# Residual gates of a two-layer hybrid diffusion step: turned to rows, kept in DRAM and read back to every partition, in place of products against the identity

## What is computed

```
for l in range(2):
    mp = split(silu(c_ctx) @ ada_w[l] + ada_b[l], 6)     # group 0: shift, scale, gate, shift, scale, gate
    ms = split(silu(c)     @ ada_w[l] + ada_b[l], 6)     # group 1
    m_p = token_mixers(modulate(xp, mp[0], mp[1]), ...)  # conv and attention, merged, @ w_out
    xp  = layer_norm(ALPHA * xp + mp[2] * m_p, ln1_g[l], ln1_b[l])
    # the same for xs with ms
    f_p = swiglu(...) if l == 0 else moe_swiglu(...)     # of modulate(xp, mp[3], mp[4])
    xp  = layer_norm(ALPHA * xp + mp[5] * f_p, ln2_g[l], ln2_b[l])
```

## Time and profile before

| | us |
|---|---|
| median of 3 runs (lowest, highest) | 1244.71 (1243.43, 1245.07) |
| the profiled execution, whole | 1244.88 |
| its span, first to last instruction | 1243.1 |
| PE busy in the span | 1142.6 |
| DVE, ACT, POOL busy | 853.1, 714.9, 127.9 |
| mean granted TensorE clock, share of full | 0.961 |

### The profile page before, as it was taken

How to read it: one execution, slowest core, us unless ns; L and a number is a source line. 1 busy time by engine, 2 the same in 40 slices (tenths; PEclk the granted TensorE clock), 3 DMA queues, 4 the chain that set the end, 5 groups by cost and what they waited for, 6 DMA issues and landing times.

```text
span 1243.1 us, 15877 instructions
## 1 busy us (share of the span) xinstructions
PE 1142.6 (92%) x5645; PEld 906.7 (73%) x5645; DVE 853.1 (69%) x1203; ACT 714.9 (58%) x1022; POOL 127.9 (10%) x132
## 2 busy tenths in 40 slices
PE   5699999999899999899999999469999999999980
PEld 1466667888788888766667887458888888888870
DVE  1575657756575455696657666449889889889965
ACT  1444445644644444544445644348888888888862
POOL 5030000001270000440000001240000000000001
PEclk7799999999999999999999999779999999999995
DMA  9799986554369656478775644079999999999952
GB/s 329 280 365 330 319 315 237 203 170 136 119 201 412 233 185 188 137 269 300 262 265 194 227 145 132 5 277 366 374 379 384 377 381 384 372 384 381 377 203 101
DMA packets 165849, 332.57 MB, mean 268 GB/s; under 512 B 6528, under 2 KB 27120, under 8 KB 165792
## 3 DMA queue, kind: packets, MB, share of 16 engines
q1 hardware_dynamic: 158288, 307.78, 70.2%
q0 software_dynamic: 7472, 24.03, 5.7%
q10 hardware_dynamic: 32, 0.01, 0.0%
HBM read 314.48 MB, written 17.30 MB: 267 GB/s over the span
## 4 chain that ended last, share of the span: by engine, by line
PE 84%; ACT 5%; DVE 4%; DMA 3%; issue 2%; POOL 0%; ACTq 0%; SPq 0%; DVEq 0%; POOLq 0%
PE bank L1302 24%; PE bank L1304 23%; PE bank L1303 23%; PE bank L1497 4%; ACT w_hi L556 2%; DMA raw<-in_ada_w 1%; PE bank L1560 1%; PE bank L1392 1%; PE bank L1578 1%; DVE xT_lo L873 1%; PE bank L1452 1%; PE bank L1568 1%; ACT work L574 1%; DVE w_lo L838 1%; ACT xT_hi L579 1%
## 5 line engine op out<-in xcount | busy, mean ns | idle before, releaser
L838 DVE TENSOR_TENSOR w_lo<-raw,w_hi 128x1024 fp32r<-128x1024 f32 (+1 forms) x492 | 571.4, 1190 | 195.7 <-ACT w_hi L556 193.7
L556 ACT ACTIVATE w_hi<-raw 128x1024 fp32r<-128x1024 f32 (+1 forms) x504 | 500.7, 1008 | 314.6 <-PE bank L1304 314.5
L1302 PE MATMUL bank<-w_hi,xT_hi 128*128 128x512 f32 (+1 forms) x1056 | 414.3, 392 | 18.4 <-DVE w_lo L838 12.3
L1304 PE MATMUL bank<-w_lo,xT_hi 128*128 128x512 f32 (+1 forms) x1056 | 402.8, 381 | 0.0
L1303 PE MATMUL bank<-w_hi,xT_lo 128*128 128x512 f32 (+1 forms) x1056 | 402.1, 381 | 0.0
L1302 PEld LDWEIGHTS bank<-w_hi,xT_hi 128*128 128x128 f32 x1056 | 200.1, 190 | 62.4 <-issue 14.2
L1304 PEld LDWEIGHTS bank<-w_lo,xT_hi 128*128 128x128 f32 x1056 | 198.9, 188 | 35.8
L1303 PEld LDWEIGHTS bank<-w_hi,xT_lo 128*128 128x128 f32 x1056 | 199.5, 189 | 30.8
L1302 PE MATMUL bank<-w_hi,hT_hi 128*128 128x512 f32 x360 | 141.7, 394 | 0.0
L1304 PE MATMUL bank<-w_lo,hT_hi 128*128 128x512 f32 x360 | 140.6, 390 | 0.0
L1303 PE MATMUL bank<-w_hi,hT_lo 128*128 128x512 f32 x360 | 140.3, 390 | 0.0
(11 more groups left out here) (234 smaller groups left out, 897.9 us busy)
## 6 DMA issues: line engine op xcount, KB each, us to landing
raw<-in_w_in SPq DMA_DIRECT2D x52, 1024.0 KB, 7.3
raw<-in_ada_w SPq DMA_DIRECT2D x48, 1024.0 KB, 7.6
raw<-in_moe_w_gate SPq DMA_DIRECT2D x32, 1024.0 KB, 7.3
raw<-in_moe_w_up SPq DMA_DIRECT2D x32, 1024.0 KB, 7.9
raw<-in_moe_w_down SPq DMA_DIRECT2D x32, 1024.0 KB, 7.7
raw<-in_moe_w_gate SPq DMA_DIRECT2D x16, 768.0 KB, 8.6
raw<-in_moe_w_up SPq DMA_DIRECT2D x16, 768.0 KB, 7.2
raw<-in_moe_w_down SPq DMA_DIRECT2D x16, 768.0 KB, 7.6
```

The source lines that it names most:

```text
L556: nc.scalar.activation(w_hi[:, unit, 0:n], raw[:, r, at:at + n], ACT.Copy).then_inc(hi_done, 1)
L838: V.tensor_tensor(w_lo[:, unit, 0:n], raw[:, r, at:at + n], w_hi[:, unit, 0:n].bitcast(F32), ALU.subtract).then_inc(lo_done, 1)
L1302: pe.matmul(o, hi, wh, start=start, stop=False)
L1304: return pe.matmul(o, hi, wl, start=False, stop=stop)
```

## The change

The gate columns of a layer are turned once, by four products with the eight columns of `adaT` of one vector and one group as the stationary operand (8x128 out, all four into bank 0). ACT copies the 8x512 result to `ada_rows[0:8, 0, :]`. POOL writes it to a new DRAM tensor `gate_rows` (four rows of 1024 for a layer), waits for that, and reads each row back to all 128 partitions of its `gate_bc` tile: two reads for n = 2l when the keys and values are stored, two for n = 2l + 1 when `merged` has come twice. DVE's two residual steps wait for these reads in place of the ACT copies. The waits of PE for the ACT copies go, and `turn_merged` waits once for the copy of bank 0.

```diff
+        gate_rows = nc.dram_tensor("gate_rows", [2 * DEPTH, G, D], F32, kind="Internal").ap()
@@ POOL, in each layer, behind load_ln(2 * l + 1) and ahead of rests(...)
+                pool.wait_ge(gate_row, l + 1)
+                pool.dma_start(gate_rows[2 * l:2 * l + 2].rearrange("n g (k d) -> k n g d", d=P),
+                               ada_rows[0:KD, 0, :].rearrange("k (n g d) -> k n g d", n=2, d=P)).then_inc(gate_kept, 16)
+                pool.wait_ge(gate_kept, 16 * (l + 1))
+                pool.wait_ge(kv_kept, 64 * (l + 1))
+                for n in (2 * l, 2 * l + 1):
+                    if n % 2:
+                        pool.wait_ge(merged, 2 * l + 2)
+                    for g in range(G):
+                        pool.dma_start(gate_bc[n % 2][g], gate_rows[n, g:g + 1, :].to_broadcast([P, D])).then_inc(gate_in[n % 2], 16)
@@ ACT
-            def gate_broadcast(n):
-                for i in range(4):
-                    act.wait_ge(bc_mm, 4 * n + i + 1)
-                    nc.scalar.activation(gate_bc[n % 2][i // 2][:, (i % 2) * COL:(i % 2 + 1) * COL], bank[i][:, :], ACT.Copy)\
-                        .then_inc(bc_ok, 1)
+            def gates_in_rows(l):
+                act.wait_ge(gate_t, l + 1)
+                nc.scalar.activation(ada_rows[0:KD, 0, :], bank[0][0:KD, :], ACT.Copy).then_inc(gate_row, 1)
@@ DVE, residual_norm and expert_residual_norm
-                dve.wait_ge(bc_ok, 4 * (n + 1))
+                dve.wait_ge(gate_in[n % 2], 16 * G * (n // 2 + 1))
@@ PE
-            def gate_broadcast(n):
-
-                pe.wait_ge(ada_kept, (4, 4, 6, 6)[n])
-                for i in range(4):
-                    for k in range(4):
-                        col = adaT[:, n // 2, 2 + 3 * (n % 2), 4 * (i % 2) + k, i // 2:i // 2 + 1]
-                        ins = pe.matmul(bank[i][:, k * P:(k + 1) * P], col.to_broadcast([P, T]), ident[:, :],
-                                        start=True, stop=True)
-                    ins.then_inc(bc_mm, 1)
+            def gates_turned(l):
+
+                pe.wait_ge(ada_kept, (4, 6)[l])
+                for i in range(2):
+                    for g in range(G):
+                        ins = pe.matmul(bank[0][0:KD, (G * i + g) * P:(G * i + g + 1) * P], adaT[:, l, 2 + 3 * i, :, g], ident[:, :],
+                                        start=True, stop=True)
+                ins.then_inc(gate_t, 1)
@@ PE, in each layer
-                gate_broadcast(2 * l)
+                gates_turned(l)
...
-                gate_broadcast(2 * l + 1)
                 rows_by_group(q0 + 1, 2, xT_hi, xT_lo, 4, 8)
                 q0 += 2
-                pe.wait_ge(bc_ok, 4 * (2 * l + 2))
```

More of the change, by code:

```diff
@@ L213, in program @@
         merged, m_t, m_hi, m_ok = (sem(n) for n in ("merged", "m_t", "m_hi", "m_ok"))
-        bc_mm, bc_ok = sem("bc_mm"), sem("bc_ok")
+        gate_t, gate_row, gate_kept = sem("gate_t"), sem("gate_row"), sem("gate_kept")
+        gate_in = [sem("gate_in0"), sem("gate_in1")]
         g_silu, h_ok, hT_t, hT_hi_ok, hT_ok = (sem(n) for n in ("g_silu", "h_ok", "hT_t", "hT_hi_ok", "hT_ok"))
@@ L778, in _ @@
                 hi(q0 + 1, 0)
-                act.wait_ge(kv_kept, 64 * (l + 1))
-                gate_broadcast(2 * l)
+                gates_in_rows(l)
                 hi(q0 + 1, 1, (0, 1, 2))
@@ L1623, in turn_merged @@
                         pe.wait_ge(merged, 2 * l + i // 2 + 1)
-                        pe.wait_ge(bc_ok, 8 * l + i + 1)
+                        if i == 0:
+                            pe.wait_ge(gate_row, l + 1)
                         for k in range(4):
```

## The result

The changed kernel takes 1232.1 us in the median of four runs (1231.82 to 1232.16), beside 1244.89 for the kernel before (1243.43 to 1245.08): 12.8 us less, a ratio of 0.9899, 95% interval 0.9882 to 0.9916. The forecast was 1232.4. The profiled execution took 1232.15 us, its span is 1230.3 against 1243.1.

The account below looks back on a forecast made before the run. PE was taken to bound the kernel: 6.98 us a layer removed less 0.80 added gives 6.18, 12.36 in all, so 1244.88 becomes 1232.5, and 1232.4 by the median. Own range 1229.5 to 1235.5; 8 in 10, 1229 to 1237.

Parts of the forecast that it names:

- What bounds the kernel: PE, busy 92% and full around the gate products: each microsecond taken from it is the kernel's; ACT's copies count nothing.
- Removed, 6.98 us a layer: On PE, two `gate_broadcast` calls a layer go, 3.49 us each, 13.96 us in all.
- Added, 0.80 us a layer (0.82 as the upper end): On PE, four new products of eight records a layer, priced like line 1618's eight, 1.60 us in all.
- Steps on POOL's queue: DRAM write 4.5 us, two issues of 0.55, second read 7.8: gates there near 283, 13 us of slack.
- Any excess over the slack is lost whole: At DVE's first residual step, gates later than the 13 us of slack cost all the excess, once a layer.
- first rival: Gates reach DVE late through POOL's DRAM write and read back, 10.4 us a layer: 1253 us; chance 5%.
- Late next: At `rows_by_group`'s fourth unit, DVE's remainder is tightest: 1.6 us of slack for PE, DVE itself just free.
- The clock: Granted clock's level in layer 1's tail and at the experts' start may shift: 3 us to both sides.
- The second: Rival: DVE late for `rows_by_group`'s fourth unit; half of 3.49 us twice lost gives 1236, all 1239.4; chance 7%.
- the third: Rival: added 2.1 MB a layer pushes the weight transfers, 5 to 6 us a layer onto PE, 1244; chance 4%.

Follow-up runs that it names:

- e2: Changed kernel with eight unneeded ACT copies of 128x512 a layer put back, four at either old place: 1232.5 us, ratio 0.9904.
- e1: The change for each layer's second sum alone, the first sum keeping its sixteen products and ACT copies: 1239.3 us, ratio 0.9959.
- e4: Changed kernel with 16 extra unused products at each of four places, stationary and moving columns 8 or 128: one execution, 1247.27 us.
- e3: Changed kernel with the write of the gate rows to DRAM repeated twelve times, each waited for: 1259.8 us, ratio 1.0129.
- e5: Changed kernel with the write of the gate rows to DRAM repeated eight times, each waited for: 1241.91 us, ratio 0.9983.
- e6: Changed kernel without the four products and ACT copy, POOL writing gate columns straight to DRAM in 4-byte pieces: 1228.88 us, ratio 0.9874.
- e7: Kernel before with 14 idle products in each of PE's two gaps of layer 1's tail: 1241.92 us, ratio 0.9981.
- e8: Changed kernel with 14 idle products in each of PE's two gaps of layer 1's tail: 1229.8 us, ratio 0.9885.

## Why the prediction was right

**What bounds the kernel.** Right. What was removed on PE came off the span, and of 10.4 us of ACT work put back 0.01 us counted in layer 0 and 0.27 in layer 1 (e2). ACT's part was put at nothing; it is 0.3 us.

**Removed, 6.98 us a layer.** Right: nothing is left at the second place, and e1 priced both places separately.

**Added, 0.80 us a layer (0.82 as the upper end).** Mis-sized: 1.06, outside my ends. The records themselves cost 0.97 us (268.61 to 269.58), 0.12 each, and 0.09 more stand ahead of the group, where the next start came 0.32 us after the last in place of 0.23. Four records of the same shape in e1 cost 0.63, so about 0.2 us are fixed and 0.108 a record. Where the fixed part comes from is open; no run isolated it. The miss is 0.5 us of the 12.4. The rule of the Trainium skill that I weighed there ("TensorE: Matmul & The Clock Gate", section "LDWEIGHTS (loading the stationary operand)"), that the time of a load goes with its columns, gave an estimate of 0.45 us together with that page's spacing for 128 moving columns, 134 cycles. That estimate did not hold for these float32 products: e4 shows 0.112 us a record with 8 stationary columns, twice the page's 0.056. My reading of line 1506 was one-sided. That 128 stationary columns pace a product with 8 moving ones did not mean that 128 moving ones are cheap.

**Steps on POOL's queue.** Right in order, too dear in size. The write released POOL after 2.2 us where I had 4.5, and the gates were there by 280.8 where I had 283. The fixed cost of about 2.0 us in the Trainium skill, "DMA: Bandwidth & Descriptors", section "Anatomy of one DMA", is close to the 1.9 us landing here. Under weight traffic the same step took up to 5.9 us (e3).

**"Any excess over the slack is lost whole".** Wrong by 5.1 us, found twice (e3, e5). I had looked at the first thing that DVE does with the gates and not at the three waits that follow it, for PE's second half, for ACT and beside POOL. It changes no number of the forecast, only where the first rival would have begun to decide.

**Late next.** Right: the fourth remainder ended 2.5 us behind the start of `rows_by_group` (293.42 and 295.94), PE did not wait for it and came 1.56 us later where I had 1.6, and DVE had 0.48 us to spare where I had written "just free".

**The clock.** Rightly kept as a term without a sign: it gave about 1.0 us, inside the 3. That the median came within 0.3 us of the forecast is in part luck: the new products cost 0.5 us more than I had put, ACT and the clock gave 0.3 and 1.0 that the sum did not have, the wait for the first expert's rows took up to 0.4 back, and the four runs of the kernel before differ by 1.65 us among themselves.

**Rivals.** None happened. The first was forced by e3, DVE 17.3 us late in layer 0, and came to 1259.8. The second did not occur: PE had no wait ahead of the fourth unit. Of the third, the added 2.1 MB a layer, nothing shows: up to layer 0's tail the change gained all that its PE rows say (6.03 against 5.9).

## What to carry to other kernels

Where one engine is busy all through a stretch, price an edit by the distance of starts around its instructions, and then look for what each neighbour must have ready; here that gave each layer's gain to 0.15 us (6.03 for 6.18). A small tensor that many partitions need went through DRAM here at no cost, since the way took 10 us (270.56 to 280.8) and its first use lay 26 us behind the start; how much lateness would hurt is read from what its consumer waits for next, not only from when it is first due. Before an edit's last microsecond is explained, hold the clock still in both kernels: its level can fall otherwise on the same work. And read a price only from records that ran at one level.

## What the hardware showed that I had not expected

- Plain float32 products against the identity cost 0.108 to 0.112 us a record at the high level whenever either side has 128 columns, and 0.028 with 8 on both (e4).
- The granted clock fell to 0.50 under a group of float32 products with 8 moving columns, although PE never waited, and the products behind it started 0.43 us apart in place of 0.23 (e4).
- A DVE step of 128x1 lasted 1.78 to 2.05 us and ended with POOL's remainder to 0.02 us, before and after the change in both layers; with POOL done it took 0.16 (e5).
- Four transfers of 1024 numbers of 4 bytes each stretched the landing of the 1 MB halves on the other queue from 5.0 to 18.5 us in the median (e6), though they move 16 KB.
- Behind an equal idle time of 3.76 us the same eight transposes ran at the high level in one kernel (1.09 us) and at the low one in another with the same PE instructions (1.97 us, e2). Idle products in the gap kept them at 1.09 us (e7, e8).
